# A two-block transformer kernel: the router computed on the turned residual, its credits given at the program's head, and three turning steps of one mixed projection made one slot later

## The reference, cut to what matters

```
# even layer: one input projection for two kinds of attention
h = rms_norm(x, norm_mix) * (1 + sc_m) + sh_m
fq, fk, fv, fgl, sq, sk, sv = _split(h @ w_in, EVEN_SPLITS)
log_f = jax.nn.log_sigmoid((fgl + forget_b))     # its running sum goes into the scores of fq, fk
sq, sk -> apply_rope                             # sliding window heads

# odd layer, after its attention
x = x + g_m * (o.reshape(B, S, -1) @ w_out)
h = rms_norm(x, norm_ffn) * (1 + sc_f) + sh_f
logits = h @ router_w + router_b                 # 8 experts
top_vals, top_idx = lax.top_k(logits, 2)
gates = softmax(top_vals)
for e in range(8): out += combine[:, e] * swiglu(h, w_gate[e], w_up[e], w_down[e])
```

## Time and profile before

| quantity | value |
|---|---|
| median of 3 runs | 1592.19 us (1591.77 to 1597.0) |
| the profiled execution: its own time | 1593.47 us |
| the profiled execution: its span | 1591.7 us |
| PE busy | 1474.8 us (93%) |
| DVE busy | 1243.5 us (78%) |
| ACT busy | 914.5 us (57%) |
| granted PE clock, mean | 0.964 |
| DMA | 358.16 MB, mean 225 GB/s |

### The profile page before, as it was taken

The page is one execution under the profiler, slowest core; times in us unless marked ns, Lnnn a source line. Parts: engine busy times, 40 slices in busy tenths (PEclk is TensorE's granted clock), DMA queues, the critical chain, the costliest instruction groups (busy, mean ns, idle before and its releaser), DMA issues.

```text
span 1591.7 us, 19806 instructions
## 1 busy us (share of the span) xinstructions
PE 1474.8 (93%) x7210; PEld 1204.2 (76%) x7211; DVE 1243.5 (78%) x1728; ACT 914.5 (57%) x1201; POOL 5.1 (0%) x17
## 2 busy tenths in 40 slices
PE   7999999997999998888999998868799999999995
PEld 5888888885888877766888887646688778878883
DVE  6758889767668797777787886794788888898887
ACT  6556663546556653565433334553577777777674
POOL 0000000000000000000000000000000000000000
PEclk9999999999999998998999998977899999999997
DMA  9654448863444465633576783212388888889882
GB/s 355 233 226 159 146 173 333 304 245 121 161 183 159 183 246 205 261 136 132 196 274 234 290 308 125 88 53 80 140 333 308 319 307 324 314 301 325 304 322 93
DMA packets 53416, 358.16 MB, mean 225 GB/s; under 512 B 6096, under 2 KB 7120, under 8 KB 12640
## 3 DMA queue, kind: packets, MB, share of 16 engines
q1 hardware_dynamic: 52736, 354.77, 59.9%
q0 software_dynamic: 176, 2.13, 0.4%
q10 hardware_dynamic: 432, 0.30, 0.1%
HBM read 356.13 MB, written 1.05 MB: 224 GB/s over the span
## 4 chain that ended last, share of the span: by engine, by line
PE 67%; DVE 18%; ACT 7%; issue 6%; DMA 1%; PEldq 0%; DVEq 0%; PEld 0%; ACTq 0%; SPq 0%
PE ps L434 20%; PE ps L436 19%; PE ps L435 19%; DVE wlo L1470 6%; ACT whi L1022 3%; PE ps L883 2%; PE ps L592 1%; DVE tok L2131 1%; PE ps L526 1%; PE ps L643 1%; DVE attn_scratch L1799 1%; DVE tok L1718 1%; DMA raw<-stream_dram 1%; ACT attn_scratch L1212 1%; DVE acc L1493 1%
## 5 line engine op out<-in xcount | busy, mean ns | idle before, releaser
L1470 DVE TENSOR_TENSOR wlo<-raw,whi 128x2048 fp32r<-128x2048 f32 (+2 forms) x304 | 651.2, 2165 | 148.6 <-ACT whi L1022 135.7
L1022 ACT ACTIVATE whi<-raw 128x2048 fp32r<-128x2048 f32 (+2 forms) x304 | 547.2, 1818 | 239.1 <-PE ps L436 233.9
L434 PE MATMUL ps<-whi,xhi 128*128 128x512 f32 (+3 forms) x1360 | 536.5, 394 | 22.0 <-DVE wlo L1470 9.2
L436 PE MATMUL ps<-whi,xlo 128*128 128x512 f32 (+3 forms) x1360 | 524.5, 386 | 0.0
L435 PE MATMUL ps<-wlo,xhi 128*128 128x512 f32 (+3 forms) x1360 | 523.7, 385 | 0.0
L434 PEld LDWEIGHTS ps<-whi,xhi 128*128 128x128 f32 x1360 | 258.4, 190 | 83.1 <-issue 13.3
L436 PEld LDWEIGHTS ps<-whi,xlo 128*128 128x128 f32 x1360 | 257.9, 190 | 52.4
L435 PEld LDWEIGHTS ps<-wlo,xhi 128*128 128x128 f32 x1360 | 258.5, 190 | 47.1
L434 PE MATMUL ps<-whi,ahi 128*128 128x512 f32 x440 | 177.3, 403 | 5.3 <-DVE wlo L1470 5.2
L436 PE MATMUL ps<-whi,alo 128*128 128x512 f32 x440 | 173.8, 395 | 0.0
L435 PE MATMUL ps<-wlo,ahi 128*128 128x512 f32 x440 | 173.7, 395 | 0.0
(11 more groups left out here) (273 smaller groups left out, 1186.5 us busy)
## 6 DMA issues: line engine op xcount, KB each, us to landing
raw<-stream_dram SPq DMA_DIRECT2D x317, 1024.0 KB, 5.3
raw<-stream_dram SPq DMA_DIRECT2D x32, 512.0 KB, 4.5
attn_scratch<-toep_dram POOLq DMA_DIRECT2D x1, 2048.0 KB, 9.3
raw<-stream_dram SPq DMA_DIRECT2D x2, 528.0 KB, 4.9
h<-x_dram SPq DMA_DIRECT2D x2, 512.0 KB, 4.7
y<-tok SPq DMA_DIRECT2D x2, 512.0 KB, 2.6
head_scratch<-w_s_dram SPq DMA_DIRECT2D x1, 512.0 KB, 13.8
head_scratch<-vg_dram SPq DMA_DIRECT2D x1, 512.0 KB, 10.9
```

Source lines behind the costliest of these rows:

```text
L434: pe.matmul(o, xh, wh, start=start, stop=False)
L436: return pe.matmul(o, xl, wh, start=False, stop=stop)
L1022: act.activation(whi[:, q % SPL, 0:w], raw[:, s % RAW, 0:w], ACT.Copy).then_inc(sem("hi_done"), 1)
L1470: dve.tensor_tensor(wlo[:, q % SPL, 0:w], raw[:, s % RAW, 0:w], whi[:, q % SPL, 0:w].bitcast(F32), ALU.subtract).then_inc(sem("lo_done"), 1)
```

## The change

**The router.** The residual itself is turned, not its normalised form. Scale and shift of the norm go elsewhere: DVE multiplies the router's weights with the scale (`rws`), PE multiplies the shift with the router's weights once (`route_shift`, into bank 4 beside the logits), and the token's own factor `1/rms` is applied to the finished logits on DVE. The first four feature blocks are turned and multiplied within the output projection's last two slots; the other four behind it. ACT makes the normalised `TA` that the gather reads. The small DVE steps are taken for both tiles at once, and the gates are computed behind the places. Three semaphore credits move from the router to the head of DVE's program; `iota` counts from 1, so that one subtraction goes. The counts of tokens per expert get a bank and a semaphore of their own. `hidden(0)` waits for each half of the gathered tokens apart (also in all 8 turns of the loop).

**The mixed projection.** `sums` and the turning of the window queries stand behind slot 1 of their chunks, the turning of the window keys behind slot 0 of the fifth. ACT takes the fourth chunk out of PSUM before it copies the turned window queries.

```diff
@@ DVE and GpSimd, head of the program
-            g.iota(iotai[:, :], [[1, P]], base=0, channel_multiplier=0).then_inc(sem("pool"), 1)
+            g.iota(iotai[:, :], [[1, P]], base=1, channel_multiplier=0).then_inc(sem("pool"), 1)
+            for name in ("g_taken", "x_tr_free", "x_tok"):
+                dve.sem_inc(sem(name), 1)
+            link(dve.tensor_scalar(experts[:, :], iota[:, 0:NE], -1.0, None, ALU.add))
@@ PE, mixed projection
             def sums(j):
-                if j == 0:
+                if j == 1:
             def window_heads(j):
-                if j == 0:
+                if j == 1:
                     pe.wait_ge(sem("kd_ready"), 1)
                     rounds([te_of(E_SQ + n * P) for n in range(4)])
-                else:
-                    rounds([(lambda t, j=j: kd[:, t, j]...) for j in range(2)], first=2)
             def fox_heads(j):
                 if j == 0:
+                    rounds([(lambda t, j=j: kd[:, t, j]...) for j in range(2)], first=2)
                     pe.wait_ge(sem("fox_ready"), 1)
@@ PE, router
-            attention(ODD, "o_out", SM_O, PT_O)
-            norm_tail(TA)
...
-            pe.wait_ge(sem("rw_landed"), 16)
+            def route(t, blocks):
+                for k in blocks:
+                    m = pe.matmul(ps[:, 4 + t, 0:NE], xT_c[:, k, t * P:(t + 1) * P], rws[:, k, :], start=k == 0, stop=k == KT - 1)
+                return m
+            def route_shift(j):
+                lead(2)(j)
+                if j == 0:
+                    pe.wait_ge(sem("rw_landed"), 16)
+                    for k in range(KT):
+                        m = pe.matmul(ps[:, 4, NE:2 * NE], shf2[:, 1, 1, k:k + 1].to_broadcast([P, P]), rw[:, k, :],
+                                      start=k == 0, stop=k == KT - 1)
+                    m.then_inc(sem("rt_add"), 1)
+            def route_half(j):
+                if j == 1:
+                    pe.wait_ge(sem("rws"), 2)
+                    pe.wait_ge(sem("tr_free"), T("tr"))
+                    for t in range(NT):
+                        route(t, range(4))
+            attention(ODD, "o_out", SM_O, PT_O, route_shift, route_half)
             for t in range(NT):
-                for k in range(KT):
-                    m = pe.matmul(ps[:, 5, t * NE:(t + 1) * NE], xT_c[:, k, t * P:(t + 1) * P], rw[:, k, :], ...)
-            m.then_inc(sem("router"), 1)
-            pe.wait_ge(sem("logits_taken"), 1)
+                pe.wait_ge(sem("h_added"), NT * 6 + t + 1)
+                for k in range(4):
+                    m = pe.transpose(ps[:, 6 + t, k * P:(k + 1) * P], h[:, t, (4 + k) * P:(5 + k) * P], ident[:, :])
+                m.then_inc(sem("tr"), 1)
+                T.up("tr")
+            for t in range(NT):
+                pe.wait_ge(sem("tr_free"), T("tr", 1 - t))
+                route(t, range(4, KT)).then_inc(sem("router"), 1)
             pe.wait_ge(sem("member"), 1)
...
+            pe.wait_ge(sem("tokens"), NT)
@@ PE, hidden(j, i)
+                    if j == 0:
+                        pe.wait_ge(sem("xg_ready"), T.up("x_s"))
@@ ACT, mixed projection
+            take(by_head(te[:, :, E_FK:E_FV]), heads=8)
             copies([sqT[:, 0:2, :], sqT[:, 2:4, :]], scale=DH ** -0.5)
-            take(by_head(te[:, :, E_FK:E_FV]), heads=8)
@@ ACT, router
-            residual()
-            stats(h)
-            tail(xT_c, scl2[:, 1, 1, :], shf2[:, 1, 1, :])
+            act.activation(st[:, 26:27], ones[:, 0:1], ACT.Sqrt)
+            used[0] += 2
+            split(used[0] + AHEAD)
+            next_pair()
+            used[0] += 2
+            split(used[0] + 1)
+            next_pair()
+            tail(xT_c, rounds=(0, 1))
+            act.wait_ge(sem("h_half"), T.up("h_half"))
...
+            for t in range(NT):
+                square(t, 0)
+            for t in range(NT):
+                act.wait_ge(sem("h_added"), T.up("h_added"))
+                square(t, 1)
+                act.wait_ge(sem("tr"), T.up("tr"))
+                act.activation(xT_c[:, 4:KT, t * P:(t + 1) * P], ps[:, 6 + t, :]..., ACT.Copy).then_inc(sem("tr_free"), 1)
+            act.wait_ge(sem("ms"), T.up("ms"))
+            act.activation(st[:, 4:6], st[:, 2:4], ACT.Sqrt).then_inc(sem("rms"), 1)
+            act.wait_ge(sem("rt_rinv"), 1)
+            for t in range(NT):
+                act.activation(TA[:, t, :], h[:, t, :], ACT.Copy, scale=st[:, 6 + t:7 + t]).then_inc(sem("tokens"), 1)
+            split(used[0] + AHEAD)
             act.wait_ge(sem("g2"), 1)
             act.activation(g2[:, :, 1], g2[:, :, 0], ACT.Exp).then_inc(sem("g2_act"), 1)
@@ DVE, router
-            residual(0)
-            normalise(h, TA)
+            dve.tensor_tensor(rws, rw[:, :, :], scl_of, ALU.mult).then_inc(sem("rws"), 1)
+            chunk()
...                                  (adds of the first half, split of one slot)
+            dve.wait_ge(sem("rt_add"), 1)
+            dve.tensor_tensor(rt_add, ps[:, 4, NE:2 * NE], rows[:, R_RB:R_RB + NE], ALU.add).then_inc(sem("rws"), 1)
...                                  (adds of the second half, 1/rms)
+            for t in range(NT):
+                dve.wait_ge(sem("router"), t + 1)
+                m = dve.scalar_tensor_tensor(rt_logit[:, t, :], ps[:, 4 + t, 0:NE], st[:, 6 + t:7 + t], rt_add, ALU.mult, ALU.add)
+            link(m)
+            for t in range(NT):
+                m = dve.max(mx8[:, t, :], rt_logit[:, t, :])
+            link(m)
+            for t in range(NT):
+                m = dve.max_index(ix8[:, t, :], mx8[:, t, :], rt_logit[:, t, :])
+            link(m)
+            link(dve.tensor_copy(idxf[:, :, :], ix8[:, :, :]))
+            dve.tensor_tensor(cb, each, of(0), ALU.is_equal)
+            link(dve.tensor_tensor(eqe[:, :, :], each, of(1), ALU.is_equal))
+            dve.tensor_tensor(member[:, :, :], cb, eqe[:, :, :], ALU.add).then_inc(sem("member"), 1)
             dve.tensor_tensor(g2[:, :, 0], mx8[:, :, 1], mx8[:, :, 0], ALU.subtract).then_inc(sem("g2"), 1)
+            link(dve.memset(macc, 0.0))
+            link(dve.tensor_copy(GT, macc[:, :, 0:P]))
+            dve.wait_ge(sem("ranks"), 1)
+            link(dve.tensor_tensor(pl, ps[:, 4, 32:48]..., member[:, :, :], ALU.mult))
+            for t in range(NT):
+                m = dve.tensor_scalar(G[:, t, :], iota[:, :], place[:, t, 0:1], None, ALU.is_equal)
+            m.then_inc(sem("places"), 1)
             dve.wait_ge(sem("g2_act"), 1)
...                                  (gates and counts, 11 small steps, then the split of one slot)
@@ DVE, split_gathered
-                    m = dve.tensor_tensor(xlo[:, k, 0:P], xg[:, k, :], xhi[:, k, 0:P].bitcast(F32), ALU.subtract)
-                m.then_inc(sem("xg_ready"), 1)
+                    dve.tensor_tensor(xlo[:, k, 0:P], xg[:, k, :], xhi[:, k, 0:P].bitcast(F32), ALU.subtract)\
+                        .then_inc(sem("xg_ready"), 1)
```

More of the change, by code:

```diff
@@ L659, in gate_blocks, with attention @@
                 return after
-            def attention(units, name, sm, pT, after=None):
+            def attention(units, name, sm, pT, after=None, mid=None):
                 n = len(units) // 2
@@ new lines, in _ @@
+            for t in range(NT):
+                pe.wait_ge(sem("tr_free"), T("tr", 1 - t))
+                route(t, range(4, KT)).then_inc(sem("router"), 1)
+            pe.wait_ge(sem("member"), 1)
+            pe.matmul(ps[:, 4, 32:32 + NE], tri[:, :], member[:, 0, :], start=True, stop=True)
+            pe.matmul(ps[:, 4, 40:40 + NE], ones[:, :], member[:, 0, :], start=True, stop=False)
+            pe.matmul(ps[:, 4, 40:40 + NE], tri[:, :], member[:, 1, :], start=False, stop=True).then_inc(sem("ranks"), 1)
@@ L874, in _ @@
+            pe.matmul(ps[:, 3, 0:NE], ones[:, :], member[:, 0, :], start=True, stop=False)
+            pe.matmul(ps[:, 3, 0:NE], ones[:, :], member[:, 1, :], start=False, stop=True).then_inc(sem("counts"), 1)
+            pe.wait_ge(sem("tokens"), NT)
             T.n.update(x_acc=0, x_tr=0, x_g=0, x_y=0, x_s=0, x_a=0, x_gt=0)
@@ new lines, in _ @@
+            m.then_inc(sem("h_half"), 1)
+            dve.wait_ge(sem("h_half"), T.up("h_half"))
+            dve.sem_inc(sem("acc_free"), 1)
+            used[0] += 2
+            split(used[0] + 1)
+            pr_ = next_pair()
+            dve.wait_ge(sem("rt_add"), 1)
+            dve.tensor_tensor(rt_add, ps[:, 4, NE:2 * NE], rows[:, R_RB:R_RB + NE], ALU.add).then_inc(sem("rws"), 1)
+            dve.wait_ge(sem("sq"), T.up("sq", 2))
+            link(dve.tensor_scalar(st[:, 28:30], st[:, 0:2], 1.0 / D, EPS, ALU.mult, ALU.add))
@@ L2142, in _ @@
             with dve.Fori(0, NE) as i:
-                T.loop(i, x_xg=2, x_silu=6, x_hi=6, x_a=6, x_y=2, y_hi=1, dve=2, xg_ready=1, x_tr=0)
+                T.loop(i, x_xg=2, x_silu=6, x_hi=6, x_a=6, x_y=2, y_hi=1, dve=2, xg_ready=2, x_tr=0)
                 product(0, i)
@@ L2184, in _ @@
                         dve.drain()
```

(2 more changed lines are left out.)

94 lines of the change are left out of this document (45 added, 49 removed).

## The result

| kernel | median us | range | runs |
|---|---|---|---|
| before | 1593.56 | 1591.77 to 1597.0 | 4 |
| changed | 1575.09 | 1571.26 to 1576.27 | 4 |

Ratio 0.9883, 95% interval 0.9868 to 0.9899: 18.5 us faster, where 19.4 were forecast. The profiled execution of the changed kernel took 1576.27 us, the slowest of its four, with a span of 1574.4; against the profiled one of before, span for span, 17.3 us are gone.

The account below looks back on a forecast made before the run. PE was taken to bound the kernel, with 67% of the chain of waits. Router 15.1 plus mixed projection 5.1 less 0.8 for the expert loop gave 19.4 us gone, so 1572.8 us; own range 1570 to 1576, wider range 1568.5 to 1578.5.

Parts of the forecast that it names:

- second tile's add to logits: Router, behind the output projection: logits at 1103.7 against 1111.87, 8.2 us gone if the clock is still full.
- gather to first matmul: Router's end: waiting only for the gather's first half leaves 6.4 us, 1.8 gone, at the low clock.
- router: Logits, membership, gather and first matmul together: 15.1 us gone, bounds 13.0 to 16.1.
- mixed projection: PE waits of 1.48 and 3.67 us and slow work go, 2.0 given back to ACT's copies: 5.1 us gone.
- first expert turn: Expert loop's first turn: DVE's first product comes 0.85 us late, so PE waits about 0.5 once.
- second wait per turn: `hidden(0)` in 8 expert turns: the extra wait costs only its issue, 0 to 0.1 us each, 0.3 taken.
- rival B: Router and mixed projection: clock stays full or copies don't stall; 22.9 us gone, 1569.3 us; chance 0.08.
- what would show it: Signs in the trace for right or wrong, among them the first expert matmul 20 us behind the last projection matmul.
- upper bound of 7.1: Mixed projection: 7.1 us gone if no stall on ACT's copies is given back.
- A: Router, mixed projection and expert turns: larger stalls and a falling clock leave 14.5 us gone, 1577.7 us; chance 0.17.
- C: Expert loop: the weight stream bounds it, only the mixed projection's 5.1 us remain at most, 1587 to 1592; chance 0.03.
- D: First expert: PE stays on the low clock, 0.43 us per matmul instead of 0.22, slower, up to 1625 us; chance 0.03.

Follow-up runs that it names:

- e2: The kernel before with only the mixed projection's changes, including the window keys' turning moved into the fifth chunk; 1588.34 us, ratio 0.9973.
- e6: The changed kernel with the clear of the expert sum and its copy moved behind the places; 1571.8 us, ratio 0.9872 to the kernel before.
- e1: The changed kernel with the mixed projection as before; 1578.65 us, ratio 0.9914 to the kernel before.
- e5: The changed kernel with 3, 6 and 8 unread products filling PE's three pauses in the router; 1573.0 us, ratio 0.9874 to the kernel before.
- e3: The changed kernel with one ACT weight split moved ahead of the window keys' copy; 1570.61 us, ratio 0.9870 to the kernel before.
- e4: The changed kernel with the expert loop's head waiting for both gather halves at once again; 1577.56 us, ratio 0.9907 to the kernel before.
- e7: The changed kernel with the first half of the logits behind the first tile's turns, outside the projection; 1571.98 us, ratio 0.9864 to the kernel before.
- e11: The changed kernel with the earlier ACT weight split and 3, 6 and 8 unread products in PE's router pauses; 1570.33 us, ratio 0.9861 to the kernel before.
- e9: The changed kernel with the earlier ACT split, the logits' first half behind the first tile's turns, and 6 and 8 unread products; 1570.99 us.

## Why the prediction was right, step by step

| term | forecast | measured |
|---|---|---|
| PE work inside the projection | +4.5 | +4.55 |
| second tile's add to logits | 8.2 gone | 8.1 (now 3.91, by the sum 3.9) |
| logits to membership | 1.67 left | 1.62 |
| membership to gather | 3.5 left | 3.37 |
| gather to first matmul | 6.4 left | 6.61 |
| router | 15.1 gone | 15.0 |
| mixed projection | 5.1 gone | 3.9 (5.5 in e2 and e6, where the clock stays full) |
| first expert turn | 0.5 lost | 1.4 |
| second wait per turn | 0.3 lost | 0 (turn 55.00) |

*The whole.* The mechanisms came as forecast but for a low clock behind the new wait, and the time lies 2.3 us above the forecast, inside its range. Part of that nearness is luck. The median says 18.5 us gone, but the two profiled executions differ by 17.3, of which 1.0 lies ahead of the mixed projection, so the parts that the forecast speaks of give 16.3 where it had 19.4.

*Router.* The sum held term by term, and e1's 13.8 bears it out (15.0 less the turn's 1.4 is 13.6). The choice of the full clock up to the logits was right (1.00 to 1099.8), and so was the low clock at the gather's head. It lasted beyond it: the half took 3.79 instead of 3.60. DVE was ready in time with more cover than the 0.85 us of the sum: it waited 1.72 for ACT's first half, since the deferred steps took 1.5 us and not 2.0. So at the full clock (e5) the first expert matmul gained 1.7 and not the 1.0 that the sum let through; what is late there is DVE, by 1.08. One pause was misread in rival B: PE's longest in the router was 5.74 us (ahead of the ranks), not 6.4; it is 1.71 now. One line of what would show it was wrongly worded: the 20 us count from the old end at 1095.3, from the new one the same sum gives 15.5, which is the 15.51 measured. The load for the gates' Exp starts at 1102.97 and the next activation at 1104.27, 0.02 behind its end. The Trainium skill (ScalarE: Activation LUTs, What ACT_TABLE_LOAD costs) counts a drain of about 1380 ns more; no trace here shows one, and the measurement decides.

*Mixed projection.* Both waits went, and the one given back was foretold with its place and cause: 1.90 us of waits measured, of which e3 takes away all but 0.45, and 2.0 forecast. Mis-sized was the term beside it: I counted no low clock behind the new wait, though the wait of 3.67 that the change removes had one, which I did count as gained. It cost 1.6 us. The upper bound of 7.1 without a stall has its counterpart in e3, which gains 6.9 here. The low clock stands behind the wait in four of six traces and in none of the five without it, so the wait is a risk and not a rule.

*First expert turn.* The stall of 0.84 on DVE's split is the one foretold at 0.5. The turn lost 1.4 in all (33.45 to 34.87); counted from start to start 1.07 of it is at the stall, and the rest comes in steps of 0.04 to 0.14 us over 17 us, whose cause stays open. e4, which starts later, has no stall. But e1, e3 and e5 have none either, and PE waits 0.9 to 1.1 us for DVE ahead of the first matmul in them; their turns take 33.9 to 34.1. So what was lost in the turn would partly have been waited for ahead of it.

*Rivals.* Of A, the 1.5 for the expert turns came (1.4), and the mixed projection gave less than 5.1, though by a low clock behind the stall and not by a longer stall; the router kept its 15.0, where A had 13.0. The time lies between the forecast and A, a little nearer the forecast (1575.1 between 1572.8 and 1577.7). B fell with the clock at the gather. C fell: the turn is 55.00 us as before, and what was saved ahead of the loop was kept. D fell: PE was back at the full clock by the first expert matmul, whose successors start 0.23 apart; e4 shows the mechanism on a small scale.

The times themselves vary by more than the last misses: the changed kernel's four runs lie 5 us apart, and their mean clocks go with them (0.974 in the fastest, 0.970 to 0.971 in the others).

## What to carry to other kernels

When work is moved forward on one engine, look at which instruction of another engine's fixed order now stands ahead of its consumer: here one weight split ahead of the copies cost 1.5 us in every trace that had it and 3.1 where the clock fell behind the wait, and moving it into idle time was one line. Count a wait with the clock behind it, both when it is removed and when it is added. Before one trace is read against another, look at how far the stages scatter that neither edit touches: here the same router code differed by 1.4 us and the same 380 us ahead of it by 3. A chain of small dependent steps is worth taking apart even where no engine is busy in it: each step can be priced from rows of its like, and the sum here held to 0.1 us in 15, with terms off by up to 0.2 that cancel.

## What the runs showed of the hardware

- After a pause of 1.65 us amid sparse turns, eight 512-column matmuls ran at the 1.2 GHz level in the changed kernel (0.52 over 681 to 684); with pauses of 0.25 and 0.20 (e3) the same place had 1.00.
- Kernels with the same pause need not get the same clock: it fell in four (changed, e4, e5, e7) and stayed at 1.00 in two (e2, e6).
- Filled pauses kept the clock at 1.00 up to the gather where it was still full when they began (e5, e11); where it had fallen (e9), the filling stood in the way: a pass of 128 columns cost 0.13 us in e5 and 0.24 in e9.
- The idle 0.37 us ahead of the 128x2048 clear belongs to that instruction. In e6 it moved with it (0.38 at its new place, 2.6 us behind the membership instead of 0.4); its cause stays open.
